# A first mixer with its gate chunks behind the scores, and attention weights split behind the units

## What is computed

```python
q, k, v, ig, fg, og = split(h @ w_in)         # 8 heads, q and k 64 wide, v 128 wide
log_i = ig + b_if[0]
log_f = log_sigmoid(fg + b_if[1])
...                                           # stabilised mLSTM, num and den per head
h_out = num / maximum(abs(den), exp(-m_t))
h_out = rmsnorm(h_out, g_head)
return (h_out * sigmoid(og)) @ w_out
```

## Time and profile before

| what | us |
|---|---|
| median of 3 runs | 1425.95 (1423.46 to 1428.09) |
| the profiled execution, whole | 1420.71 |
| its span | 1419.0 |
| PE busy in the span | 1320.9 |
| DVE busy | 900.3 |
| ACT busy | 622.8 |

### The profile page before, as it was taken

One profiled execution on the slowest core, in us unless ns is written; L12 is line 12 of the kernel. 1 busy time (PEld: TensorE's weight loads), 2 busy tenths in 40 slices (PEclk: granted clock), 3 DMA queues, 4 the chain that ended last, 5 costly groups with the idle time before them and its releaser, 6 DMA issues.

```text
span 1419.0 us, 16722 instructions
## 1 busy us (share of the span) xinstructions
PE 1320.9 (93%) x6795; PEld 1112.2 (78%) x6795; DVE 900.3 (63%) x1365; ACT 622.8 (44%) x876; POOL 27.7 (2%) x35
## 2 busy tenths in 40 slices
PE   5999999968999999999999976999999999989887
PEld 4888888957788888878888764778888999868765
DVE  6655558875655557685856485465555584577665
ACT  5444346414444345544443464354434343434431
POOL 1000000110000000000000000000000000000000
PEclk9999999968999999999999998999999999999899
DMA  8655546313455555547564230155555775156001
GB/s 278 210 178 178 180 148 237 121 58 114 153 178 178 188 199 174 174 159 235 178 220 155 89 107 0 62 176 185 196 183 149 156 227 172 45 166 237 30 1 60
DMA packets 158636, 217.66 MB, mean 153 GB/s; under 512 B 8208, under 2 KB 110944, under 8 KB 158560
## 3 DMA queue, kind: packets, MB, share of 16 engines
q1 hardware_dynamic: 156848, 212.56, 46.6%
q0 software_dynamic: 1232, 3.18, 0.7%
q10 hardware_dynamic: 480, 0.85, 0.2%
HBM read 215.52 MB, written 1.05 MB: 153 GB/s over the span
## 4 chain that ended last, share of the span: by engine, by line
PE 81%; DVE 13%; ACT 3%; issue 2%; DMA 1%; ACTq 0%; POOL 0%; DVEq 0%
PE PS L650 22%; PE PS L651 22%; PE PS L653 22%; DVE wlo L1934 3%; DVE xs L2210 1%; PE PS L767 1%; PE PS L681 1%; PE PS L682 1%; PE PS L1223 1%; PE PS L670 1%; ACT whi L1437 1%; PE PS L688 1%; PE PS L966 1%; DVE arena L2455 1%; PE PS L1408 1%
## 5 line engine op out<-in xcount | busy, mean ns | idle before, releaser
L1934 DVE TENSOR_TENSOR wlo<-raw,whi 128x2048 fp32r<-128x2048 f32 (+3 forms) x207 | 459.5, 2231 | 129.5 <-ACT whi L1437 128.8
L650 PE MATMUL PS<-whi,XL 128*128 128x512 f32 (+3 forms) x992 | 389.1, 393 | 22.4 <-DVE wlo L1934 9.2
L1437 ACT ACTIVATE whi<-raw 128x2048 fp32r<-128x2048 f32 (+3 forms) x207 | 383.1, 1867 | 58.6 <-DMA raw<-in_fox_w_in_dram 33.7
L651 PE MATMUL PS<-wlo,XH 128*128 128x512 f32 (+3 forms) x992 | 382.6, 386 | 0.0
L653 PE MATMUL PS<-whi,XH 128*128 128x512 f32 (+3 forms) x992 | 265.9, 385 | 0.0
L650 PEld LDWEIGHTS PS<-whi,XL 128*128 128x128 f32 x992 | 189.0, 191 | 59.0 <-DVE wlo L1934 9.9
L651 PEld LDWEIGHTS PS<-wlo,XH 128*128 128x128 f32 x992 | 189.3, 191 | 33.1
L653 PEld LDWEIGHTS PS<-whi,XH 128*128 128x128 f32 x992 | 186.5, 191 | 35.8
L1491 ACT ACTIVATE scr<-PS,rn 128x256 f32<-128x256 f32 x88 | 41.8, 474 | 226.6 <-PE PS L653 223.9
L650 PE MATMUL PS<-whi,GL 128*128 128x512 f32 x320 | 125.4, 392 | 0.0
L651 PE MATMUL PS<-wlo,GH 128*128 128x512 f32 x320 | 124.6, 389 | 0.0
(11 more groups left out here) (360 smaller groups left out, 1474.0 us busy)
## 6 DMA issues: line engine op xcount, KB each, us to landing
raw<-in_ffn_w_in_dram SPq DMA_DIRECT2D x176, 512.0 KB, 4.8
raw<-in_ffn_w_out_dram SPq DMA_DIRECT2D x88, 512.0 KB, 4.8
raw<-in_fox_w_in_dram SPq DMA_DIRECT2D x24, 512.0 KB, 7.9
raw<-in_a_w_in_dram SPq DMA_DIRECT2D x16, 512.0 KB, 4.7
raw<-in_dsa_w_in_dram SPq DMA_DIRECT2D x16, 512.0 KB, 5.3
raw<-in_kv_w_dram SPq DMA_DIRECT2D x12, 512.0 KB, 4.3
raw<-in_fox_w_in_dram SPq DMA_DIRECT2D x12, 344.0 KB, 5.2
raw<-in_a_w_out_dram SPq DMA_DIRECT2D x8, 512.0 KB, 4.5
```

Source lines behind the costliest of these rows:

```text
L650: mm(o, xl, wh, start=start and i == 0, stop=False, skip_group_check=True)
L651: mm(o, xh, wl, start=False, stop=False, skip_group_check=True)
L1437: A(whi[:, p % SLOTS, 0:n], raw[:, p % SLOTS, 0:n], ACT.Copy).then_inc(hi_done, 1)
L1934: V.tensor_tensor(wlo[:, p % SLOTS, 0:n], raw[:, p % SLOTS, 0:n], whi[:, p % SLOTS, 0:n].bitcast(F32), ALU.subtract).then_inc(lo_done, 1)
```

## The change

- The chunks of the mixer are ordered gates and 256 gate columns, values, values, q, k, and then the two chunks of 384 output-gate columns. The last two are no longer ordinary chunks: `og_products` does them one tile at a time, the first tile's between scores and numerators, the second tile's behind the last numerators. ACT takes the sigmoid straight out of the bank.
- The running sum is kept as b_sum plus b_rest, and the floor and a are shifted by DEEP = 9, so that the sigmoid s is small and s * (1 + s) stands for s / (1 - s): one instruction of DVE in place of three. The rest comes in again as a factor per token in `m_weights`, now two instructions a head.
- Scores and numerators go in groups of four heads; one division, one square and one sum for four heads.
- The head's gain is loaded as a broadcast row by POOL and multiplied into the gate by DVE; XH and XL of `mlstm_out` are then made a whole bank at a time. DVE makes XL of tile 0 between the heads of tile 0 and those of tile 1.
- The four pieces of the mixer's output weight are split at named places between these steps.
- Attention: the last projection piece is split before q is evicted; the two splits inside the units are moved behind the last unit.

```diff
-        "mlstm": (a["a_w_in"][0], [(A_CHUNK, 2048, 272), (A_CHUNK, 2320, 384), (A_CHUNK, 2704, 384),
-                                   (A_CHUNK, 1024, 512), (A_CHUNK, 1536, 512), (B_CHUNK, 0, 512), (B_CHUNK, 512, 512)]),
+        "mlstm": (a["a_w_in"][0], [(A_CHUNK, 2048, 272), (A_CHUNK, 1024, 512), (A_CHUNK, 1536, 512),
+                                   (B_CHUNK, 0, 512), (B_CHUNK, 512, 512), (A_CHUNK, 2320, 384), (A_CHUNK, 2704, 384)]),
...
+            pool.wait_ge(params_in, 16 * 9)
+            pool.wait_ge(par_ready, 2)
+            pool.dma_start(m_gain, a["a_g_head"].rearrange("l h d -> l (h d)")[0:1, :].to_broadcast([P, D])).then_inc(gain_in, 16)
...
-            for name, row in (("m_a", grow[0]), ("m_floor", grow[1])):
+            for name, sums in (("m_a", (grow[2], grow[0])), ("m_floor", (grow[1],))):
                 o = side(name)
                 pe.wait_ge(side_src, src_no[name])
-                for t in range(NT):
-                    last = tr(o[:, 8 * t:8 * t + 8], row[:, t * P:t * P + P], con[0:HEADS, 0:HEADS])
+                for i, row in enumerate(sums):
+                    for t in range(NT):
+                        last = tr(o[:, 16 * i + 8 * t:16 * i + 8 * t + 8], row[:, t * P:t * P + P], con[0:HEADS, 0:HEADS])
                 last.then_inc(side_ps, 1)
...
+            def og_products(c, t, bank):
+
+                n, end = stages["mlstm"][1][c][2], chunk_end("mlstm", c)
+                for i, p in enumerate((end - 2, end - 1)):
+                    if t == 0:
+                        pe.wait_ge(lo_done, p + 1)
+                    wh, wl = parts_n(p, 4, n)
+                    last = product(PS[:, bank, 0:n],
+                                   [(XH[:, 4 * i + k, t * P:t * P + P], XL[:, 4 * i + k, t * P:t * P + P],
+                                     wh[:, k, :], wl[:, k, :]) for k in range(4)], start=i == 0, stop=i == 1)
+                    if t == 1:
+                        last.then_inc(used, 1)
+                if t == 0:
+                    last.then_inc(og_ps, 1)
+
+            pe.wait_ge(chunk_act, first_chunk["mlstm"] + 5)
+            pe.wait_ge(chunk_dve, first_chunk["mlstm"] + 5)
             pe.wait_ge(ones_ready, 1)
-            for hh in range(2):
+            for hh in range(4):
                 m_scores(hh)
-            for hh in range(HEADS):
-                if hh + 2 < HEADS:
-                    m_scores(hh + 2)
+            pe.wait_ge(side_act, looks(side_no["m_M3"], "act"))
+            og_products(5, 0, 7)
+            for hh in range(4):
                 m_numerator(hh)
+            for hh in range(4, 8):
+                m_scores(hh)
+            pe.wait_ge(m_out, 1)
+            og_products(6, 0, 7)
+            for hh in range(4, 8):
+                m_numerator(hh)
+            og_products(5, 1, 2)
+            og_products(6, 1, 3)
...
+            def og_in(c, t, bank):
+
+                at, n = m_og_at[c]
+                if t == 0:
+                    act.wait_ge(og_ps, c - 4)
+                else:
+                    act.wait_ge(used, chunk_end("mlstm", c))
+                A(m_og[:, t, at:at + n], PS[:, bank, 0:n], ACT.Sigmoid, scale=rn[:, t:t + 1]).then_inc(og_act, 1)
+
+            def head_squares(g, to):
+
+                act.wait_ge(m_out, g + 1)
+                A(to, xs[:, :, 512 * g:512 * g + 512], ACT.Square).then_inc(head_sq, 1)
+
+            og_in(5, 0, 7)
+            head_squares(0, m_squares[0])
+            split_to(first + 3)
+            og_in(6, 0, 7)
+            head_squares(1, m_squares[1])
+            og_in(5, 1, 2)
+            og_in(6, 1, 3)
+            split_to(first + 4)
...
+            split_to(first + 5)
             q_in(0, 0)
             q_in(0, 1)
-            split_to(first + 5)
             gates_in(0)
             split_to(first + 7)
...
-                elif k == KVH + 2:
-                    split_to(first + 8)
-                elif k == KVH + 4:
-                    split_to(first + 9)
                 elif k == len(n_units) - 2:
                     cmp_out(1, 2 * (k % 2))
+            split_to(first + 9)
             n_z(1)
...
+                link(V.tensor_tensor(q, e, sq, ALU.add))
+                link(V.tensor_tensor(e, q, e, ALU.subtract))
+                link(V.tensor_tensor(rest, sq, e, ALU.subtract))
...
+            b_sum, b_rest = xs[0:HEADS, 0, 0:T], xs[0:HEADS, 0, T:2 * T]
+            log_forget(0, "m_rows", b_rest)
+            link(V.tensor_tensor(grow[2], grow[0], b_sum, ALU.subtract))
+            link(V.tensor_tensor(grow[1], grow[2], b_sum, ALU.add))
+            link(V.tensor_tensor(grow[0], grow[0], grow[1], ALU.subtract))
+            V.tensor_tensor(grow[0], grow[0], b_rest, ALU.subtract).then_inc(side_src, 1)
+            link(V.tensor_tensor_scan(grow[3], zcol[0:HEADS, :].to_broadcast([HEADS, T]), grow[2], 0.0,
                                       ALU.add, ALU.max))
-            V.tensor_tensor(grow[1], grow[2], grow[3], ALU.add).then_inc(side_src, 1)
+            link(V.tensor_tensor(grow[1], b_sum, grow[3], ALU.add))
...
+            values_in(2)
             o = odd_bank("mlstm", 3)
-            V.tensor_scalar(m_v[:, 1, 0:4, 0:P], o.rearrange("p (h d) -> p h d", h=4), r2[:, 1:2], None, ALU.mult).then_inc(chunk_dve, 1)
+            V.tensor_copy(m_qT[:, 2:4, :], two(o)).then_inc(chunk_dve, 1)
             o = side("m_a")
-            V.tensor_copy(m_a, o[:, 0:16].rearrange("p (t h) -> p t h", t=NT)).then_inc(side_dve, 1)
-            o = odd_bank("mlstm", 4)
-            V.tensor_scalar(m_v[:, 1, 4:8, 0:P], o.rearrange("p (h d) -> p h d", h=4), r2[:, 1:2], None, ALU.mult).then_inc(chunk_dve, 1)
+            V.tensor_scalar(m_rest, o[:, 16:32].rearrange("p (t h) -> p t h", t=NT), 0.125, 0.125, ALU.mult, ALU.add)
+            V.tensor_scalar(m_a, o[:, 0:16].rearrange("p (t h) -> p t h", t=NT), -DEEP, None, ALU.add).then_inc(side_dve, 1)
+            dve.wait_ge(side_dve, looks(side_no["m_a"], "dve"))
 
             def decay(j):
 
-
                 dve.wait_ge(side_act, looks(side_no[f"m_M{j}"], "act"))
-                sg = m_E[:, 2 * j:2 * j + 2, :]
-                rest = xs[:, j % 2, 0:768].rearrange("p (h t) -> p h t", h=2)
-                link(V.tensor_scalar(rest, sg, 0.75, -1.0, ALU.min, ALU.add))
-                link(V.reciprocal(rest, rest))
-                V.scalar_tensor_tensor(out=sg, in0=sg, scalar=-1.0, in1=rest, op0=ALU.mult, op1=ALU.mult).then_inc(m_decay, 1)
+                deep = m_E[:, 2 * j:2 * j + 2, :]
+                V.scalar_tensor_tensor(out=deep, in0=deep, scalar=1.0, in1=deep, op0=ALU.add, op1=ALU.mult)\
+                    .then_inc(m_decay, 1)
...
-                V.scalar_tensor_tensor(out=m_E[:, hh, :], in0=PS[:, hh % 4, 0:384], scalar=0.125, in1=m_E[:, hh, :],
-                                       op0=ALU.mult, op1=ALU.mult).then_inc(m_w, 1)
+                V.scalar_tensor_tensor(out=m_E[:, hh, 0:T], in0=PS[:, hh % 4, 0:T], scalar=m_rest[:, 0, hh:hh + 1],
+                                       in1=m_E[:, hh, 0:T], op0=ALU.mult, op1=ALU.mult)
+                V.scalar_tensor_tensor(out=m_E[:, hh, T:384], in0=PS[:, hh % 4, T:384], scalar=m_rest[:, 1, hh:hh + 1],
+                                       in1=m_E[:, hh, T:384], op0=ALU.mult, op1=ALU.mult).then_inc(m_w, 1)
...
+            def numerators_in(g):
+
+                dve.wait_ge(m_num, 4 * g + 4)
+                o = PS[:, 4:8, :].rearrange("p h (t n) -> p h t n", t=NT)
+                den = o[:, :, :, 128:129].rearrange("p h t n -> p h (t n)")
+                rd = m_tok[:, 32 + 8 * g:40 + 8 * g].rearrange("p (h t) -> p h t", h=4)
+                floor = m_floor[:, :, 4 * g:4 * g + 4].rearrange("p t h -> p h t")
+                link(V.scalar_tensor_tensor(out=rd, in0=den, scalar=-1.0, in1=floor, op0=ALU.mult, op1=ALU.max))
                 link(V.tensor_tensor(rd, rd, den, ALU.max))
                 link(V.reciprocal(rd, rd))
+                V.tensor_tensor(xs[:, :, 512 * g:512 * g + 512].rearrange("p t (h d) -> p h t d", h=4), o[:, :, :, 0:P],
+                                rd.unsqueeze(3).to_broadcast([P, 4, NT, P]), ALU.mult).then_inc(m_out, 1)
+
+            def head_sums(g):
+
+                dve.wait_ge(head_sq, g + 1)
+                sums = ss[:, 0:16].rearrange("p (t h) -> p t h", t=NT)[:, :, 4 * g:4 * g + 4]
+                link(V.tensor_reduce(sums, m_squares[g].rearrange("p t (h d) -> p t h d", h=4), AX, ALU.add))
+
+            def og_gain(t):
+
+                dve.wait_ge(og_act, 2 * t + 2)
+                dve.wait_ge(gain_in, 16)
+                V.tensor_tensor(m_og[:, t, :], m_og[:, t, :], m_gain, ALU.mult).then_inc(og_dve, 1)
+
...
+            split_to(first + 1)
+            for hh in range(4):
+                m_weights(hh)
+            split_to(first + 2)
+            numerators_in(0)
+            for hh in range(4, 8):
+                m_weights(hh)
+            head_sums(0)
+            split_to(first + 3)
+            og_gain(0)
```

(59 more changed lines are left out.)

94 lines of the change are left out of this document (40 added, 54 removed).

## The result

The changed kernel takes **1382.76 us** (median of 4 runs, 1382.46 to 1393.33) against 1426.33 for the kernel before (4 runs, 1423.46 to 1428.09). The ratio is 0.9715, with a 95% interval of 0.9688 to 0.9742: 2.9% faster, or 40.6 us by that ratio of all runs. The two medians lie 43.6 apart, as one of the four changed runs took 1393.33. The forecast was 1390, in a range of 1379 to 1407. The profiled execution took 1382.88 us for a span of 1381.2; before it was 1420.71 for 1419.0. Of the versions run later, two had one execution each far above the rest (1883 and 3321 us), and the kernel before had one (1919 us); the medians leave these out.

What follows compares the result with a forecast made beforehand. PE bounds the whole run, but VectorE's reciprocals the first mixer's chain. Mixer 16.3, attention start 5.5 and units 14.0 make 35.8 us off 1420.71: 1384.9; with 5.2 for the median, 1390, range 1379 to 1407.

Steps and rivals of the forecast that it cites:

- the log's chain: Mixer, VectorE's log of the forget gates: starts 2.7 us earlier, ends at 244.9, as before.
- the gain in order: Mixer: the new chunk order starts the log 2.7 us earlier; six added instructions cost 2.7.
- The new stall: Mixer, before m_M0: PE idles 5.2 us behind VectorE's copy of m_a; the clock falls, price 3.3 us.
- pieces 10 and 11 (to 254.5): Mixer, VectorE: two pieces ahead of the q copy and m_a's copy, ending at 254.5; a whole piece costs 2.24 us.
- What was costed at nothing: Gain's broadcast, later landings of pieces 17 to 20, and pieces split before tile 1's z behind the attention units: no cost.
- The start: Attention's start: the early split cuts PE's wait from 3.39 to about 1.1 us; 5.5 gained, bounds 2.3 and 5.5.
- if the short wait spares the clock: Attention's start: condition under which up to 3.2 us more are gained on the products behind the wait.
- The next three units: Attention: without splits and lower clock, three units take 11.6 us, not 25.7; 14.0 gained, bounds 11.4 and 14.3.
- Uncovered gates: Rival, mixer: 16.6 us of gate products stand on the path; mixer gives 5.4, total 1401; chance 0.10.
- The slower case: Lower clock holds from the stall at 250 to the output stage and in the attention units: 13 us slower, 1439; chance 0.03.
- that allowance: Whole kernel: 5.2 us added because the median of runs, 1425.95, lay above the profiled execution.

Runs made afterwards that it cites:

- both orders: Changed kernel with VectorE's copy of m_a ahead of pieces 10 and 11 and the q eviction, and tile 1's transposes inside the output stage: 1382.06 us, again 1383.93.
- stall removed: Changed kernel with VectorE's copy of m_a put ahead of pieces 10 and 11 and the q eviction: 1383.97 us, ratio 0.9694 to the kernel before.

## Why the prediction was right, and where it was off

**Chain by chain in the mixer.** The stages up to the log stood where the working put them: the log's chain ended at 244.46 (244.9 predicted), so the gain in order was indeed eaten by the six added instructions. The new stall came, and the clock fell: idle 4.65 (5.2), m_M0 at 253.84 (255.4), the grant 0.50 behind it. The kernel with that stall removed prices it at 4.9, with a fall of the clock left in; where the clock stayed up (both orders) the first transposes of the heads come 7.1 earlier than in the changed kernel. All later steps ran 1.1 to 1.8 early in the same order: first gate product 274.39 (276.0), second 285.17 (286.6), last gates' end 300.63 (301.8), PE's idle ahead of tile 1 4.50 (4.8), first output product 308.63 (310.4). Up to that product the mixer gave 18.1 instead of 16.3 (326.70 to 308.63). Over its whole stretch it gave 17.6: the output stage begins at a grant of 0.51 now, and takes 0.5 longer.

The term that failed is "pieces 10 and 11 (to 254.5)": they were taken as whole pieces of 2.24, but those two slots hold the 384-column gate chunk now, 1536 columns, 1.70 each (the 3.40 for two above). That is 1.1 of the 1.8; 0.4 were there at the end of the log's chain, and the rest is rounding.

**What was costed at nothing** cost nothing: no wait on a landing at piece 17 or later, none on the gain's broadcast, none for z of tile 1 behind the units. From its first output product to the next transposes of the hidden state the attention took PE 19.16 us before and after (900.58 to 919.74, 863.81 to 882.97).

**Attention.** The start was taken at 5.5 us, the upper bound, on the step "if the short wait spares the clock". The wait shrank to 1.07 as predicted, but the grant fell all the same: 0.83 from 779.5 to 789.5. Start and first units gave 4.06 (up to the copy at 842.72), and the kernel with the old order of the split puts 4.0 of that on the start. The step that failed is the clock's: 1.7 us came back, not 3.2. The next three units gave 15.06 instead of 14.0, above the stated bound of 14.3, since one takes 3.53 and not 3.8 to 4.0. The sum of the two, 19.1, is 0.4 off 19.5; that it is so near is luck, for two errors of opposite sign lie in it.

**Rivals.** Uncovered gates would have given 1401, and the kernel that makes them uncovered has a median of 1401.79. That is a coincidence: its mixer lost 12.9 us and not the rival's 10.9 (16.3 less 5.4), and its runs reach from 1394.96 to 1408.34. The slower case needed the low clock to hold; in the mixer it held 6.5 us behind the first stall and some 5 behind the second.

**The total.** 35.8 was predicted and 37.8 measured between the two profiles: mixer 1.3 more, attention 0.4 less, and 1.1 in the rest of the kernel, where no instruction changed and which no step of the working gave. The other 5.2 of the distance from 1390 to 1382.76 were no step of the working but the allowance for the median above the profiled execution. The profile of before, 1420.71, lay below all its timed runs; the one of after, 1382.88, is at their median, so that allowance wasn't needed.

**Still open.** The experiments name the reciprocals as the largest part of the mixer's gain; that the clock's part of their price is some 8 us rests on two profiles, not on a pair that differs in the clock alone. How the 6.2 us of the new order divide among the groups of four, the place of the gate products and the output's copies wasn't measured. That the timed runs of both orders don't show the 10.3 us of their profiles isn't settled either.

## What to carry to other kernels

An operation that is slow for each element can cost in two ways when the matmul engine waits for it: by its own time, and by the lower clock behind the idle. Find work of the matmul engine that depends on nothing in the chain, and issue it between the chain's links in portions as long as a link; here that was worth 12.9 us, for 16.6 us of products. And when stages are reordered, look for the short instruction that now stands behind long ones in its queue: m_a's copy behind two splits cost 4.9 us. Before two profiles are compared, look at whether the clock fell in the same places in both.

## What the hardware showed that was not expected

**Equal instructions, two clocks.** The kernels "stall removed" and "both orders" are the same program up to the first tile's transposes. Windows of the first, then of the second, in the mixer:

```profile
248.70:251.70 3.00, 2.30 (x15) 1.85 (x14) 3.00 (x6) 1.98 (x4) 0.00 (x0) 0.96 0.95 331
251.70:258.20 6.50, 6.50 (x30) 6.04 (x29) 6.43 (x6) 4.83 (x9) 3.51 (x3) 0.50 0.32 126
```

```profile
248.70:251.70 3.00, 2.30 (x15) 1.83 (x14) 3.00 (x6) 2.02 (x4) 0.00 (x0) 1.00 0.95 297
251.70:258.20 6.50, 6.50 (x54) 6.39 (x54) 6.43 (x6) 5.13 (x10) 3.54 (x3) 1.00 0.37 138
```

PE was idle for 0.70 us in both and had a few eight-row products; in one execution the grant then fell to 0.50 (1.2 GHz) for 6.5 us, in the other it stayed at 1.00 (2.4 GHz). The price of that fall can be read from PE's timelines, again of the first and then of the second, whose mixers begin within 0.1 us of each other:

```profile
297.36 1.09 PE L705 MATMUL PS<-con,xs 128*128 128x128 f32 x8 [0.79 <-DVE xs L2330]
```

```profile
294.35 1.09 PE L705 MATMUL PS<-con,xs 128*128 128x128 f32 x8 [0.79 <-DVE xs L2329]
```

The first transposes of the heads come 3.0 us later where the clock fell, and up to there no instruction differs. The prediction had priced a fall at these rows at 3.3.

The attention shows it too. Windows that begin 36 us behind the first narrow product, in the changed kernel and in "stall removed":

```profile
815.53:827.53 12.00, 9.46 (x72) 6.39 (x72) 11.05 (x17) 7.62 (x30) 0.00 (x0) 1.00 0.00 1
```

```profile
810.64:822.64 12.00, 10.44 (x61) 7.98 (x61) 8.91 (x15) 5.97 (x30) 0.00 (x0) 0.69 0.00 0
```

Ten profiles have the attention's new instructions in the new order. Six of them took 117.1 to 118.8 us and four 123.8 to 125.8, with nothing between. In that window the six have 1.00, and the four 0.69 to 0.78. The start differs as well. Behind the same wait of 1.07 to 1.08 the grant over 10 us is 1.00 in two of the ten, among them the first profile of both orders, 0.83 in seven and 0.66 in one:

```profile
769.08:779.08 10.00, 10.00 (x60) 8.84 (x61) 5.28 (x16) 7.03 (x9) 0.00 (x0) 1.00 0.14 48
```

The two with 1.00 are the two of 117.1 and 117.2, 1.6 us below the other four of the six. So the step "if the short wait spares the clock" came true in two executions of ten. What decides it wasn't found. The Trainium skill, TensorE: Matmul & The Clock Gate, section A second HAM failure mode: psum-queue depth-cycling, describes a kernel whose frequent small idles between groups of products make the clock go to and fro. The idle of 0.70 us here is a small one too, though a single one; the section does not say that one program can have either outcome. For a change of some 5 us this is the limit of what a single profile can tell.

**A reciprocal is slow for each element.** It took 4.96 us for 768 columns, 6.5 ns each, beside 0.96 for a scalar_tensor_tensor of that shape. The Trainium skill, VectorE: DVE Perf Modes, section First, the fixed hardware budget, says that it is an iterative divide that repeats eight times; it gives no price, and the ratio here is 5.2.
